# The last chunk of a delta-rule mixer: other order of its steps, fewer key transposes, projection products between them

## The reference, cut to what matters

```python
def step(state, inp):
    r_t, d_t, k_t, v_t, a_t, b_t = inp
    sa = jnp.einsum('bhvk,bhk->bhv', state, a_t)
    state = (state * d_t[:, :, None, :] + sa[..., None] * b_t[:, :, None, :]
             + v_t[..., None] * k_t[:, :, None, :])
    return state, jnp.einsum('bhvk,bhk->bhv', state, r_t)
...
y = ((y - mu) * lax.rsqrt(var + GN_EPS)).reshape(b, s, RWKV_WIDTH) * f32(ln_w) + f32(ln_b)
bonus = jnp.sum(rh * kh * f32(r_k), axis=-1, keepdims=True) * vh
y = (y + bonus.reshape(b, s, RWKV_WIDTH)) * g
...
x = x + jnp.concatenate([out_a, out_b, out_m], axis=-1) @ w_out[l]
```

## Time and profile before

| | |
|---|---|
| Median of 3 runs | 2410.73 us (2409.45 to 2411.15) |
| The profiled execution | 2412.35 us, of which the span of its instructions 2410.5 us |
| Mean granted TensorE clock | 0.963 |
| PE busy | 2256.4 us, 94% |
| DVE, ACT, POOL busy | 1150.1 (48%), 994.3 (41%), 880.2 us (37%) |
| DMA | 85 GB/s on average |

### The profile page before, as it was taken

How to read it: one execution, slowest core, us unless ns; L and a number is a source line. 1 busy time by engine, 2 the same in 40 slices (tenths; PEclk the granted TensorE clock), 3 DMA queues, 4 the chain that set the end, 5 groups by cost and what they waited for, 6 DMA issues and landing times.

```text
span 2410.5 us, 37084 instructions
## 1 busy us (share of the span) xinstructions
PE 2256.4 (94%) x14399; PEld 1869.2 (78%) x14399; DVE 1150.1 (48%) x1944; ACT 994.3 (41%) x1685; POOL 880.2 (37%) x490
## 2 busy tenths in 40 slices
PE   4999598999999998989989999989998889999998
PEld 3888487888888886867778888877756777878877
DVE  3699824342034335678444214458445436540541
ACT  5666544332133314578454324444453213441441
POOL 1699324233223323400154444433421113444443
PEclk8999798999999998999999999999898979999999
DMA  8778011222222221300123323332200002332332
GB/s 274 254 255 274 26 53 53 61 61 73 60 61 61 71 69 55 90 26 1 44 81 97 109 85 97 106 106 79 83 1 1 2 1 71 103 101 85 98 105 83
DMA packets 337729, 205.95 MB, mean 85 GB/s; under 512 B 5997, under 2 KB 335287, under 8 KB 337591
## 3 DMA queue, kind: packets, MB, share of 16 engines
q1 hardware_dynamic: 331915, 193.83, 26.9%
q10 hardware_dynamic: 5676, 10.24, 1.4%
HBM read 200.28 MB, written 2.19 MB: 84 GB/s over the span
## 4 chain that ended last, share of the span: by engine, by line
PE 73%; issue 11%; POOL 5%; DVE 5%; ACT 3%; DVEq 1%; SPq 1%; DMA 1%; ACTq 1%; POOLq 0%
PE ps L624 21%; PE ps L625 21%; PE ps L626 21%; POOL w_lo L551 2%; POOL pc L1612 2%; PE ps L2127 1%; DVE ps L1580 1%; PE ps L897 1%; PE ps L2155 1%; ACT w_hi L594 1%; DVE m L3337 1%; PE ps L3136 1%; PE ps L3123 1%; DMA ada_x<-in_ada_w 1%; PE ps L1672 1%
## 5 line engine op out<-in xcount | busy, mean ns | idle before, releaser
L551 POOL TENSOR_TENSOR w_lo<-raw,w_hi 128x1024 fp32r<-128x1024 f32 (+1 forms) x203 | 525.9, 2592 | 1079.7 <-ACT w_hi L594 1063.1
L624 PE MATMUL ps<-x_hi,w_hi 128*128 128x512 f32 (+1 forms) x1896 | 686.1, 362 | 37.2 <-DVE x_lo L1482 14.7
L625 PE MATMUL ps<-x_lo,w_hi 128*128 128x512 f32 (+1 forms) x1896 | 675.7, 356 | 0.0
L626 PE MATMUL ps<-x_hi,w_lo 128*128 128x512 f32 (+1 forms) x1896 | 674.4, 356 | 0.0
L594 ACT ACTIVATE w_hi<-raw 128x1024 fp32r<-128x1024 f32 (+1 forms) x251 | 280.8, 1119 | 617.2 <-PE ps L626 611.8
L624 PEld LDWEIGHTS ps<-x_hi,w_hi 128*128 128x128 f32 x1896 | 364.7, 192 | 102.2 <-issue 22.7
L625 PEld LDWEIGHTS ps<-x_lo,w_hi 128*128 128x128 f32 x1896 | 365.4, 193 | 49.9 <-issue 1.7
L626 PEld LDWEIGHTS ps<-x_hi,w_lo 128*128 128x128 f32 x1896 | 364.4, 192 | 50.4
L1862 DVE SCALAR_TENSOR_TENSOR f_a<-ps,prm,f_a 128x511 f32<-128x511 f32 (+2 forms) x176 | 116.2, 681 | 378.9 <-ACT f_b L1824 368.0
L624 PE MATMUL ps<-g_hi,w_hi 128*128 128x512 f32 (+1 forms) x704 | 256.8, 365 | 3.9 <-DVE g_lo L1871 3.4
L625 PE MATMUL ps<-g_lo,w_hi 128*128 128x512 f32 (+1 forms) x704 | 255.8, 363 | 0.0
(11 more groups left out here) (395 smaller groups left out, 2967.3 us busy)
## 6 DMA issues: line engine op xcount, KB each, us to landing
raw<-in_ffn_w_up SPq DMA_DIRECT2D x88, 512.0 KB, 3.8
ada_tail<-in_ada_w SPq DMA_DIRECT2D x22, 1024.0 KB, 7.4
raw<-in_ffn_w_down SPq DMA_DIRECT2D x32, 704.0 KB, 4.6
raw<-in_w_up SPq DMA_DIRECT2D x44, 512.0 KB, 3.8
ada_s<-in_ada_w SPq DMA_DIRECT2D x20, 1024.0 KB, 7.9
raw<-in_conv_w_pw SPq DMA_DIRECT2D x24, 512.0 KB, 5.9
raw<-in_w_down SPq DMA_DIRECT2D x16, 704.0 KB, 4.6
raw<-in_w_in SPq DMA_DIRECT2D x17, 512.0 KB, 4.0
```

The costliest lines, as they stand in the source:

```text
L551: pool.tensor_tensor(M.w_lo[:, slot, 0:K * P], M.raw[:, slot, 0:K * P], M.w_hi[:, slot, 0:K * P].bitcast(F32), ALU.subtract).then_inc(lo_r ...
L624: pe.matmul(o, wh, hi[:, k, t0:t0 + tn], start=first, stop=False)
L625: pe.matmul(o, wh, lo[:, k, t0:t0 + tn], start=False, stop=False)
L626: return pe.matmul(o, wl, hi[:, k, t0:t0 + tn], start=False, stop=last)
```

## The change

Two buffers are added, `M.tok3` for the last chunk's transposed values and `M.y1b` for its turned output. The rest concerns chunk 3 and the steps of chunk 2 that stand among its levels.

- The last chunk's keys (`tok03`, `tok13`) are no longer transposed and copied; its values are, at level 2 instead of behind level 5.
- PE: `x0` of the second half is split. What it takes from values and state (`x0b_known`) runs after level 4's products, and what it takes from the first half's solution (`x0b_rest`) later. `x0(3, 0)` runs at level 5, ahead of that level's last products. `y(3)` is split into three: `y_values` behind level 5, `y_state` after the first `u`, `y_rest` at the end. It has PSUM banks 0 and 3 for its own.
- PE: the known products of the first `w_out` tile are taken apart: block 0 stands between `x0b_rest` and the second `u`, block 1 between that `u` and `y_rest`, blocks 2, 6 and 7 between `y_rest` and `turned(3)`. `turned(2)` moves from level 5 to ahead of the second `u`, into bank 1.
- DVE: `state(2)` runs at level 3 ahead of the centring of `y(2)`, both of whose other parts follow at levels 4 and 5; `gated(2)` and `low_part(2)` stand with those of chunk 3.
- ACT: `deviation(2)` follows the first copy of `x0`, `turned(2)` and `high_part(2)` stand with those of chunk 3.
- New waits on PE: `x0b_known` waits for the centring of `y(2)` on DVE (`yc2`), since it overwrites banks 6 and 7, and `state(2)` for ACT's copy of the values (`tok23`).

```diff
     def tensor_steps(n):
...
-        return out_ + [f"tok1{n}", f"tok2{n}"]
+        return out_ + ([f"tok1{n}", f"tok2{n}"] if n < 3 else ["ua3", "x0b3", "yt2", "ub3", "y3", "yt3"])
...
+        def x0b_known(n):
+
+            b, t = HALVES[1], slice(n * P + HD, (n + 1) * P)
+            S_S.after(pe, f"tok2{n}")
+            V_S.after(pe, f"st{n - 1}")
+            V_S.after(pe, f"yc{n - 1}")
+            for hh in H6:
+                pe.matmul(by_parity(hh)[b, :], M.m4[:, n % 2, hh, 2 * P + HD:3 * P],
+                          values_of(n)[:, hh * HD:(hh + 1) * HD], start=(hh < 2), stop=False, skip_group_check=True)
+            for hh in H6:
+                r, c = head_rows(hh), hh // 2
+                pe.matmul(by_parity(hh)[b, :], kk_t[c][r, t], M.z[r, c, :], start=False, stop=False,
+                          skip_group_check=True)
+
+        def x0b_rest(n):
+            b = HALVES[1]
+            S_S.after(pe, f"ua{n}")
+            for hh in H6:
+                mm = pe.matmul(by_parity(hh)[b, :], M.m4[:, n % 2, hh, HD:P], M.u[:, hh * HD:(hh + 1) * HD],
+                               start=False, stop=True, skip_group_check=True)
+            T_S.mark(mm, f"x0b{n}")
...
+                    if n == 3:
+                        tokens(3, 2)
...
-                if e == 5:
+                if e == 5 and n == 3:
+                    x0(3, 0)
+                elif e == 5:
                     if n:
                         turned(n - 1)
                     tokens(n, 0)
                 for gr, hs in GROUPS:
                     inv_step(n, e, gr, hs)
-            tokens(n, 1)
-            tokens(n, 2)
+                if n == 3 and e == 4:
+                    x0b_known(3)
+            if n < 3:
+                tokens(n, 1)
+                tokens(n, 2)
+        y_values(3)
+        V_S.after(pe, "inv503")
         V_S.after(pe, "inv513")
-        for half in (0, 1):
-            x0(3, half)
-            u(3, half)
-        y(3)
-        w_out_part(pe, 0, KNOWN)
+        u(3, 0)
+        y_state(3)
+        x0b_rest(3)
+        w_out_known(pe, 0, KNOWN[:1])
+        turned(2)
+        u(3, 1)
+        w_out_known(pe, 0, KNOWN[1:2])
+        y_rest(3)
+        w_out_known(pe, 0, KNOWN[2:])
         turned(3)
-        w_out_part(pe, 1, KNOWN)
+        w_out_known(pe, 1, KNOWN)
...
-        for half in (0, 1):
-            x0(3, half)
-            u(3, half)
-        for step in (deviation, turned, high_part):
-            step(3)
+        x0(3, 0)
+        deviation(2)
+        u(3, 0)
+        x0(3, 1)
+        u(3, 1)
+        turned(2)
+        deviation(3)
+        turned(3)
+        high_part(2)
+        high_part(3)
...
         of_last = {3: (variance,), 4: (normed, state), 5: (gated,)}
+        of_third = {3: (state, centred), 4: (spread,), 5: (normed,)}
...
-                for step in of_last.get(e, ()) if n else ():
+                for step in (of_third if n == 3 else of_last).get(e, ()) if n else ():
                     step(n - 1)
+        variance(3)
+        normed(3)
+        gated(2)
+        gated(3)
         low_part(2)
-        for step in (variance, normed, gated, low_part):
-            step(3)
+        low_part(3)
```

More of the change, by code:

```diff
@@ L3052, in of_parity, with values_of, y_place, y1_of @@
         return ap.rearrange("p (c a x) -> p a c x", c=3, a=2)[:, p, :, :]
+    def values_of(n):
+        return M.tok3 if n == 3 else M.tok[:, 2, :]
+    def y_place(n, hh):
+        if n < 3:
+            return by_parity(hh)
+        at = 3 * (hh % 2) * 512 + (hh // 2) * HD
+        return M.ps[:, at:at + HD]
+    def y1_of(n):
+        return M.y1b if n == 3 else M.y1
+    def turned_bank(n):
+        return 1 if n == 2 else 6
+    def y_bank(n, p):
+        return bank(3 * p if n == 3 else 6 + p, 192)
     STATE_AT = 256
@@ L3145, in tokens @@
                     V_S.after(pe, f"st{n - 1}")
-            else:
-                S_S.after(pe, f"tok{q_ - 2}{n}" if q_ == 2 else f"yt{n - 1}") if q_ == 2 or n else None
+            elif q_ == 2:
+                S_S.after(pe, f"tok0{n}" if n < 3 else "x0b2")
+            elif n:
+                S_S.after(pe, f"yt{n - 1}")
             for c in C3:
@@ L3164, in x0 @@
                     mm = pe.matmul(by_parity(hh)[b, :], M.m4[:, n % 2, hh, 2 * P + half * HD:2 * P + half * HD + HD],
-                                   M.tok[:, 2, hh * HD:(hh + 1) * HD], start=True, stop=(n == 0 and half == 0))
+                                   values_of(n)[:, hh * HD:(hh + 1) * HD], start=True, stop=(n == 0 and half == 0))
                 for hh in pair_ if n else ():
@@ L3172, in x0, with y_values, y_state, y_rest @@
             T_S.mark(mm, f"x0{'ab'[half]}{n}")
+        def x0b_known(n):
[17 more added lines that the diff above has]
+            T_S.mark(mm, f"x0b{n}")
+        def y_values(n):
+            for hh in H6:
+                pe.matmul(y_place(n, hh), M.m4[:, n % 2, hh, 3 * P:4 * P], values_of(n)[:, hh * HD:(hh + 1) * HD],
+                          start=(hh < 2), stop=False, skip_group_check=True)
+        def y_state(n):
+            t = slice(n * P, (n + 1) * P)
+            for hh in H6:
+                r, c = head_rows(hh), hh // 2
+                pe.matmul(y_place(n, hh), r_t[c][r, t], M.z[r, c, :], start=False, stop=False, skip_group_check=True)
+        def y_rest(n):
+            S_S.after(pe, f"ub{n}")
+            for hh in H6:
+                mm = pe.matmul(y_place(n, hh), M.m4[:, n % 2, hh, P:2 * P], M.u[:, hh * HD:(hh + 1) * HD],
+                               start=False, stop=True, skip_group_check=True)
+            T_S.mark(mm, f"y{n}")
         def u(n, half):
@@ L3183, in state @@
             S_S.after(pe, f"ub{n}")
+            if n == 2:
+                S_S.after(pe, "tok23")
             def place(hh):
@@ L3214, in turned @@
             for c in C3:
[L3215 removed]
+                mm = pe.transpose(bank(turned_bank(n), P, c * P), M.y[:, c * P:(c + 1) * P], ident)
             T_S.mark(mm, f"yt{n}")
@@ L3375, in state, with centred @@
             V_S.mark(ins, f"st{n}")
-        def variance(n):
+        def centred(n):
             T_S.after(dve, f"y{n}")
-            y_ps = [heads(bank(6 + p, 192)) for p in (0, 1)]
+            y_ps = [heads(y_bank(n, p)) for p in (0, 1)]
             for p in (0, 1):
@@ L3391, in variance @@
             V_S.mark(dve.tensor_reduce(M.gn[:, 1, :], q6, AX.X, ALU.add), f"var{n}")
+        def variance(n):
+            centred(n)
+            spread(n)
         def normed(n):
```

59 lines of the change are left out of this document (39 added, 20 removed).

## The result

The changed kernel takes 2398.54 us (median of 5 executions, 2394.58 to 2400.78) against 2411.15 us (5 executions, 2409.45 to 2415.33) for the kernel before. The ratio is 0.9943 with a 95% interval of 0.9931 to 0.9955: 12.6 us less by the medians. The forecast was 2398.3 us in a range from 2394.5 to 2405.0.

The account below looks back on a forecast made before the run. The prediction took a chain of small fp32 products on PE, partly at half clock, as the bound. Full clock saves 15.4 us, less 3.0 for a partial fall: 2410.73 - 12.4 = 2398.3 us, range 2394.5 to 2405.0.

Parts of the forecast that it names:

- the third of the prediction's signs of being wrong: Time from the late products' start to the end of the span is not the 416.65 us of before.
- The first: Sign of being wrong: the late products start outside 1978.5 to 1987.4 us.
- the full-clock case: Chunk 3's steps with the clock at 1.00 up to the late products, which then start at 1978.5 us.
- The sum at full clock: Step-by-step costs from level 2 to the late products at clock 1.00: 15.4 us saved.
- The new wait: x0b_known, between levels 4 and 5, waits for DVE's centring; level 5 starts 1.6 us late, its 1.9 us not paid later.
- a third of the half-clock loss: Clock down for part of the stretch from 1958 us: 3 us off 15.4, leaving 12.4 us saved.
- the first rival: Full clock throughout the stretch: 15.4 us saved, 2395.3 us; chance 0.22.
- The case that I gave 0.22: Full clock throughout, rival (1): 15.4 us saved, 2395.3 us.
- My counter-row: Kernel before, 1980 to 1985 us: PE busy 5.00 us of 5, clock at 0.50; cited against full clock throughout.
- Half clock throughout: Rival (2): the clock stays down until the products behind y_rest; 6.4 us saved, 2404.3 us; chance 0.20.
- a shift that is lost: Rival (3): level 5's delay grows or the saving ends at a w_out wait; within 4.8 us of before; chance 0.05.
- a slower kernel by thinly spread products: Rival (4): spread projection products no longer raise the clock, later tiles run at 0.50; -9.7 us, 2420.4 us; chance 0.03.

Follow-up runs that it names:

- e4_known_later: Changed kernel with x0b_known and its wait for the centring moved behind level 5's first products; 2400.56 us, ratio 0.995, tail 28.50 us.
- the second pair: Changed kernel unaltered and the kernel before, timed again side by side; 2398.52 us against 2409.91 us, ratio 0.9945.
- e2_old_order_blocks: Kernel before, old order, with four known blocks of the first projection tile put into PE's four bare waits; 2415.98 us, ratio 1.0001, tail 34.5 us.
- e9_old_order_clock_up: Kernel before with four first-tile blocks in PE's waits, plus three second-tile blocks ahead of x0(3, 0); 2409.81 us, ratio 0.9994, tail 34.58 us.
- e1_blocks_behind_y: Changed kernel with the two projection blocks in PE's waits moved behind y_rest; 2399.74 us, ratio 0.994, tail 25.25 us.
- e10_y_whole: Changed kernel with y(3) whole again, y_values and y_state directly ahead of y_rest; 2401.56 us, ratio 0.9956, tail 29.8 us.
- e3_no_key_turns: Kernel before without the last chunk's unused key transposes and ACT's copies of them; 2412.32 us, ratio 0.9992, tail 40.27 us.
- e6_centre_later: Changed kernel with DVE centring y(2) behind level 4's sums, and level 5 and y_values ahead of x0(3, 0) and x0b_known; 2398.29 us, ratio 0.9939.

## Why the prediction was right, and where it was not

**The direction and the bound** held. The stage is a file of small products on PE, a shift of the late products reaches the end, and the rest took 416.6 us in five of the six traces of the two kernels. In the sixth, the profiled execution of the result, it was 418.24, with a fall of the clock at the start of `w_out`. That is the third of the prediction's signs of being wrong, and it was seen here. The first was met by chance: the late products began at 1978.46 us, at the full-clock case's 1978.5, but with a tail that started 1.6 us later and was 17.0 us shorter.

**The sum at full clock** said 15.4 us. Measured, with its own term for the transposed values (0.64 us at level 2, taken as 0.4; DVE's sums of level 1 and 2 are 4.18 us apart, 3.54 before), it is 17.0 - 0.64 = 16.4 us. What I mis-sized are the products sorted by kind. I took `x0b_known` at the pair-by-pair price, 3 x (0.38 + 0.26) = 1.9 us; it took 1.2 to 1.4, since its last products overlap level 5's. `y_state` was put at 1.1 and took 0.82, `x0b_rest` at 1.14 and took 0.84, and level 5's two groups of products at 1.2 and took 0.7 to 0.9. Against that, a block cost 0.89 us and not 0.7. From the end of `y` on, the terms (4.05 us, the turn, 3.8 us) fit: 8.4 us measured, 8.5 forecast.

**The new wait** was placed right (0.99 us for the centring, level 5 at 1958.1 us), and its reading as no loss on the whole held in e4_known_later.

**The step that failed** is the clock. "I take a third of the half-clock loss, 3 us: a fall for part of the stretch" is in no trace of the changed kernel: the tail ran at 1.00 in all three, so the first rival's case was the real one. That the median still lies on the forecast is owed to something else. The gain of the tail is 16.4 us net, and two things outside it took some back in the traces: a fall in `w_out`, 1.6 us in one of three, and a later start. The changed kernel's tails start at 1952.64, 1954.26 and 1954.39 us, those of before at 1951.02, 1949.67 and 1953.00. Of this mean difference of 2.5 us the transposes explain 0.64. The rest lies nearly all ahead of level 1 of chunk 3, where the two kernels' instructions are the same; over all fourteen traces of this study DVE's first sum of that level lies anywhere from 1938.1 to 1946.2 us, 1941.5 on the mean of the six with the old order and 1941.3 of the eight with the new. That speaks for chance. It leaves open why the medians gain only 12.6 and, in the second pair, 11.4 us where the tail gains 16.4: the kernel before may keep its clock in some executions, as the traces of e2_old_order_blocks and e9_old_order_clock_up did with the same instructions up to level 5, but none of its own three traces shows it.

**The case that I gave 0.22.** My counter-row, PE busy 5.00 of 5 at 0.50, showed that `y(3)` didn't raise a clock that had fallen; it said nothing of whether a clock still up would be kept. I had read the one for the other. In the changed kernel PE was busy 5.00 of 5 from 1960 to 1970 us at 1.00, on the same kinds of product. The Trainium skill (TensorE: Matmul & The Clock Gate, Why this matters for your kernels) says to keep TensorE continuously busy for the full rate, and that gave the right case for the changed kernel. As a rule the traces don't bear it out either way: in e2_old_order_blocks the clock fell in the midst of unbroken work, and in e9_old_order_clock_up it stayed at 1.00 from 1960 to 1965 us with PE busy 2.65 us of 5.

**The rivals.** Half clock throughout, a shift that is lost, and a slower kernel by thinly spread products: none occurred. The new kernel's blocks were not what decided the clock (e1_blocks_behind_y). What the changed order does differently is seen in e4_known_later and e10_y_whole: idle time of PE put back into it (0.75 us in one place, 0.67 and 0.57 in two) came with a dip of the clock. In e1_blocks_behind_y 0.15 and 0.57 us came without one. Over all fourteen traces: of the seven with 1.49 to 1.74 us of idle time between levels 4 and 5, the clock fell behind it in five (the kernel before in all three, e3_no_key_turns, e4_known_later) and not in two (e2_old_order_blocks, e9_old_order_clock_up); of the seven with 0.18 to 1.00 us, it fell there in none. So the shorter gap between levels 4 and 5 is the likely cause that the clock stayed up. And once down ahead of the end of `y`, it was back within 4 us in e4_known_later and e10_y_whole, which is the "fall for part of the stretch" that I had forecast, but stayed down for 30 us in the kernel before. These things go together in the traces; they are not shown as a rule.

## What to carry to other kernels

Before pricing a reordering of small products, ask at which clock the stretch runs: here, by an estimate from two traces, somewhat under two thirds of the gain up to `y` came with a clock that no longer fell, and the rest with the shorter path. A row of a busy engine at half clock shows that the clock stayed down there. It doesn't show that the clock can't rise under such work (in e4_known_later it did), nor that it would fall under it. And filler work in waits is worth only what it covers: a block of 0.89 us in a wait of 0.5 lengthens the file, and belongs in the longest wait there is.

## What was not expected of the hardware

Products of two shapes cost more here where they alternate. At a clock of 1.00 and in the same trace, the 12 products of `x0(3, 0)`, two of values and two of state in turn, took 1961.13 - 1959.22 = 1.9 us; the same number in `x0b_known`, all six of values and then all six of state, took 1.2 us up to 1958.35 us, or 1.4 with its last ones, which run among level 5's. It fits that `x0b_rest` alone took 0.84 us against 3 x 0.38 within pairs. The two write other halves of the banks, and no kernel here changed the order alone, so the cause is not isolated.

Stages ahead of the change vary by more than the change is worth. The first sum of level 1 in chunk 3, up to which all kernels here issue the same instructions in this stage, came between 1938.1 and 1946.2 us, a spread of 8 us; a gain of a microsecond was to be seen in the tail's own length (same to 0.04 us) and not in medians. Such a length needs the right end: in e6_centre_later the late products did not follow `low_part`, and the 1.2 us between them are visible only by counting PE's products behind the turn.
